# A decoder block with a 16384-expert mixer on one core: gates fetched and applied one tile further ahead, exponentials between weight copies, first two router heads sooner, low parts in two halves

## What is computed

```python
q = (xc @ wq).reshape(PEER_CHUNK, PEER_HEADS, 2, PEER_QDIM // 2)
sc = jnp.einsum('thpd,pkd->thpk', q, subkeys)
sv, si = lax.top_k(sc, PEER_TOPK)
cand = sv[:, :, 0, :, None] + sv[:, :, 1, None, :]
cv, ci = lax.top_k(cand.reshape(PEER_CHUNK, PEER_HEADS, PEER_TOPK * PEER_TOPK), PEER_TOPK)
i1 = jnp.take_along_axis(si[:, :, 0], ci // PEER_TOPK, axis=-1)
i2 = jnp.take_along_axis(si[:, :, 1], ci % PEER_TOPK, axis=-1)
e = i1 * PEER_NKEYS + i2
g = jax.nn.softmax(cv.astype(jnp.float32), axis=-1)
act = jax.nn.gelu(jnp.einsum('td,thkd->thk', xc, u[e]))
return jnp.einsum('thk,thkd->td', g * act, v[e])
```

## Time and profile before

| | us |
|---|---|
| timed runs, median (lowest to highest) | 1072.34 (1070.92 to 1072.85) |
| profiled execution | 1071.63 |
| its span | 1069.6 |
| PE busy / DVE / ACT / POOL | 1047.1 / 812.1 / 629.8 / 332.5 |
| U's tiles 0 to 127 start | 269.18 to 656.24 |
| V's tile 0 starts, `last_two` starts, last matmul starts | 660.11, 1058.50, 1066.00 |

### The profile page before, as it was taken

One profiled execution on the slowest core, in us unless ns is written; L12 is line 12 of the kernel. 1 busy time (PEld: TensorE's weight loads), 2 busy tenths in 40 slices (PEclk: granted clock), 3 DMA queues, 4 the chain that ended last, 5 costly groups with the idle time before them and its releaser, 6 DMA issues.

```text
span 1069.6 us, 21135 instructions
## 1 busy us (share of the span) xinstructions
PE 1047.1 (98%) x6814; PEld 913.8 (85%) x6814; DVE 812.1 (76%) x1631; ACT 629.8 (59%) x1128; POOL 332.5 (31%) x227
## 2 busy tenths in 40 slices
PE   9999999999999999999999999999999999999998
PEld 7798899999999999999999999766676777777775
DVE  7768886788989988977667667887778876666665
ACT  5557776665455445477667666666666654444443
POOL 0011211036268777876877874000000000000000
PEclk9999999999999999999999999999999999999999
DMA  8674646665456666576766766555555576666553
GB/s 339 245 236 134 203 142 212 197 205 170 157 161 174 173 182 188 166 187 168 176 165 169 177 159 173 178 176 169 168 172 177 177 228 200 202 201 201 199 200 106
DMA packets 89473, 198.20 MB, mean 185 GB/s; under 512 B 26320, under 2 KB 42832, under 8 KB 89424
## 3 DMA queue, kind: packets, MB, share of 16 engines
q1 hardware_dynamic: 68544, 188.99, 53.6%
q0 software_dynamic: 20736, 8.46, 6.9%
q10 hardware_dynamic: 144, 0.14, 0.1%
HBM read 187.01 MB, written 10.55 MB: 185 GB/s over the span
## 4 chain that ended last, share of the span: by engine, by line
PE 57%; DVE 15%; issue 14%; ACT 11%; DVEq 1%; ACTq 1%; DMA 0%
PE bank L830 10%; PE bank L832 10%; PE bank L831 10%; ACT hi L1197 7%; DVE lo L1682 6%; DVE big L1922 3%; ACT auxh L1224 3%; PE bank L384 2%; PE bank L385 2%; PE bank L386 2%; PE bank L450 2%; PE bank L770 2%; DVE gsum L1860 2%; DVE oneA L1852 2%; PE bank L454 1%
## 5 line engine op out<-in xcount | busy, mean ns | idle before, releaser
L1682 DVE TENSOR_TENSOR lo<-raw,hi 128x1024 fp32r<-128x1024 f32 x253 | 320.6, 1271 | 100.4 <-ACT hi L1197 99.7
L1197 ACT ACTIVATE hi<-raw 128x1024 fp32r<-128x1024 f32 x253 | 266.2, 1052 | 155.4 <-PE bank L832 152.4
L830 PE MATMUL bank<-xhi,hi 128*128 128x256 f32 x1024 | 292.4, 286 | 3.5 <-DVE lo L1682 2.3
L832 PE MATMUL bank<-xhi,lo 128*128 128x256 f32 x1024 | 290.6, 284 | 0.0
L831 PE MATMUL bank<-xlo,hi 128*128 128x256 f32 x1024 | 290.4, 284 | 0.0
L2038 POOL DMA_INDIRECT gate_d<-chosen_w,chosen_at x128 | 236.2, 1845 | 73.7 <-issue 48.2
L830 PEld LDWEIGHTS bank<-xhi,hi 128*128 128x128 f32 x1024 | 197.4, 193 | 4.0 <-ACT hi L1197 3.5
L831 PEld LDWEIGHTS bank<-xlo,hi 128*128 128x128 f32 x1024 | 197.2, 193 | 0.0
L832 PEld LDWEIGHTS bank<-xhi,lo 128*128 128x128 f32 x1024 | 197.0, 192 | 0.0
L886 PE MATMUL bank<-hi,auxh 128*128 128x512 f32 x504 | 168.3, 415 | 1.8 <-DVE auxl L1915 0.4
L886 PE MATMUL bank<-lo,auxh 128*128 128x512 f32 x504 | 156.9, 392 | 0.0
(11 more groups left out here) (393 smaller groups left out, 1493.2 us busy)
## 6 DMA issues: line engine op xcount, KB each, us to landing
raw<-u_d SPq DMA_DIRECT2D x128, 512.0 KB, 3.4
raw<-v_d SPq DMA_DIRECT2D x128, 512.0 KB, 3.4
raw<-wpre_d SPq DMA_DIRECT2D x70, 512.0 KB, 4.4
gate_d<-big POOLq DMA_DIRECT2D x16, 512.0 KB, 5.4
gring<-gate_d SPq DMA_DIRECT2D x128, 64.0 KB, 3.0
big<-wpre_d SPq DMA_DIRECT2D x8, 512.0 KB, 8.3
gate_d<-chosen_w,chosen_at POOLq DMA_INDIRECT x128
big<-x_d SPq DMA_DIRECT2D x4, 256.0 KB, 4.3
```

The costliest lines, as they stand in the source:

```text
L830: pe.matmul(out, wh, xhi[:, k, :], start=(k == 0), stop=False)
L832: m = pe.matmul(out, wl, xhi[:, k, :], start=False, stop=(k == KT - 1))
L1197: act.activation(hi[:, slot(n), :], raw[:, splits(n) % RING, :], ACT.Copy).then_inc(hi_done, 1)
L1682: dve.tensor_tensor(lo[:, slot(n), :], raw[:, splits(n) % RING, :], hi[:, slot(n), :].bitcast(F32), ALU.subtract).then_inc(lo_done, 1)
```

## The change

Five edits, in the order of the diff. The exponentials move to U's steps 4, 18 and 50 and are laid between the copies: table load, high part of one tile, exponential, high part of the next, table load, then the gelu of the pair. In DVE's router order the first two heads (8 and 9) go through `choose_pairs`, `numbers`, `weights` and `addresses` ahead of `choose_keys(15)` and `choose_keys(0)`. In U's second half each low part is subtracted in two halves of 512 columns. In V `gate_block` runs for block j + 4 in step j, not j + 3, with one more block ahead of the loop. POOL scatters five columns instead of three ahead of the pair sums of heads 14 and 15, and waits for their keys only behind these.

```diff
--- before.py
+++ after.py
@@ -67,7 +67,7 @@
 HALF = NBLK // 2
 GRING = 4
 EARLY = 7
-EXP_AT = (8, 20, 51)
+EXP_AT = (4, 18, 50)
 
 
 PARAMS = dict(g2=8, qg=64, kgc=64, kgs=128, posk=16, posv=16, w2k=128, w2v=128, subk=256, gw=192)
@@ -1251,11 +1251,15 @@
             act.wait_ge(S("h_saved"), 16 * TB)
             def weights_exp(z, b, c0, c1):
 
+                j = EXP_AT[z]
                 act.preload_act_table_set(LN_EXP)
+                loop_hi(0, N_PRE + j + SPLIT)
                 act.wait_ge(S("router_d"), z + 1)
                 of_heads = gwt[:, c0 * 16:c1 * 16]
                 act.activation(of_heads, of_heads, ACT.Exp, scale=rs2[:, b:b + 1]).then_inc(S("router_exp"), 1)
+                loop_hi(0, N_PRE + j + 1 + SPLIT)
                 act.preload_act_table_set(GELU)
+                gelu_pair(0, j + 1, 0)
 
             def u_steps(j0, j1):
 
@@ -1264,11 +1268,11 @@
 
             u_steps(0, EXP_AT[0])
             weights_exp(0, 1, NH, NH + 2)
-            u_steps(EXP_AT[0], EXP_AT[1])
+            u_steps(EXP_AT[0] + 2, EXP_AT[1])
             weights_exp(1, 1, NH + 2, 2 * NH)
-            u_steps(EXP_AT[1], EXP_AT[2])
+            u_steps(EXP_AT[1] + 2, EXP_AT[2])
             weights_exp(2, 0, 0, NH)
-            u_steps(EXP_AT[2], ROUTER - 2)
+            u_steps(EXP_AT[2] + 2, ROUTER - 2)
             for j in range(ROUTER - 2, ROUTER):
                 loop_hi(0, N_PRE + j + SPLIT)
             act.wait_ge(S("bank67_read"), 2)
@@ -1800,19 +1804,19 @@
 
             keys_ready()
             spread(1)
-            choose_keys(0)
             sc_out(NH - 1)
-            spread(2)
+            choose_pairs(NH, 4)
+            from_best(NH, NH + 2)
+            numbers(NH, NH + 2, 4, 6)
+            weights(0, NH, NH + 2)
+            dve.wait_ge(S("cleared"), 16 * 16)
+            addresses(NH, NH + 2)
             dve.wait_ge(S("sc_out"), NH)
             choose_keys(2 * NH - 1)
             keys_ready()
-            spread(3)
-            choose_pairs(NH, 6)
-            from_best(NH, NH + 2)
-            numbers(NH, NH + 2, 6, 9)
-            weights(0, NH, NH + 2)
-            dve.wait_ge(S("cleared"), 16 * 16)
-            addresses(NH, NH + 2)
+            spread(8)
+            choose_keys(0)
+            spread(9)
             for z in range(3):
                 choose_pairs(NH + 2 + 2 * z, 12 + 3 * z)
             from_best(NH + 2, 2 * NH)
@@ -1883,6 +1887,14 @@
             dve.wait_ge(S("bank45_read"), NH + HALF // 2)
             dve.tensor_copy(gsum[:, 0, 0:1], eT[:, 2, 0:1]).then_inc(S("weighed"), 1)
 
+            def loop_lo_halves(i, n):
+
+                dve.wait_ge(hi_done, i * UNROLL + splits(n + 1))
+                dve.tensor_tensor(lo[:, slot(n), 0:512], raw[:, splits(n) % RING, 0:512],
+                                  hi[:, slot(n), 0:512].bitcast(F32), ALU.subtract).then_inc(S("lo_first"), 1)
+                dve.tensor_tensor(lo[:, slot(n), 512:1024], raw[:, splits(n) % RING, 512:1024],
+                                  hi[:, slot(n), 512:1024].bitcast(F32), ALU.subtract).then_inc(lo_done, 1)
+
             def u_step_g(i, j):
                 g = j // 2
                 if j % 2 == 0:
@@ -1892,7 +1904,7 @@
                     weigh(i, g, GT)
                     rows_a(i, g + 2, GT)
                 if j < HALF - 1:
-                    loop_lo(i, N_PRE + HALF + j + SPLIT)
+                    loop_lo_halves(i, N_PRE + HALF + j + SPLIT)
 
             each_tile(dve, HALF - 16, u_step_g)
             for j in range(HALF - 16, HALF):
@@ -1928,6 +1940,7 @@
             gate_block(0, 1)
             w_lo_tokens(0, 1, "whi_done", 1, "wlo_done")
             gate_block(0, 2)
+            gate_block(0, 3)
             w_lo(0, 1)
             dve.wait_ge(S("bank45_read"), NH + NBLK // 2)
             weigh(0, NGRP, GT)
@@ -1937,7 +1950,7 @@
             def v_step(i, j):
                 w_lo(i, j + SPLIT - 1)
                 loop_lo(i, V0 + j + SPLIT)
-                gate_block(i, j + SPLIT)
+                gate_block(i, j + GRING)
 
             def v_step_g(i, j, keys=True, rows=True):
                 g = NGRP + 1 + j // 2
@@ -1951,12 +1964,14 @@
                     if rows:
                         rows_a(i, g + 2, GT)
                 loop_lo(i, V0 + j + SPLIT)
-                gate_block(i, j + SPLIT)
+                gate_block(i, j + GRING)
 
             each_tile(dve, HALF - 16, v_step_g)
             for j in range(HALF - 16, HALF - 2):
                 v_step_g(0, j, keys=j < HALF - 8, rows=j < HALF - 6)
-            each_tile(dve, HALF - 1, lambda i, j: v_step(i, HALF - 2 + j))
+            each_tile(dve, HALF - 2, lambda i, j: v_step(i, HALF - 2 + j))
+            w_lo(0, NBLK - 2)
+            loop_lo(0, V0 + NBLK - 1)
             w_lo(0, NBLK - 1)
             dve.wait_ge(S("h_back"), 16 * TB)
             for z, (b, c, w) in enumerate(out_parts_v):
@@ -2044,10 +2059,10 @@
                 pair_sum(c)
             pick(NH)
             pick(NH + 1)
-            pool.wait_ge(S("keys_chosen"), 2)
             pool.wait_ge(S("router"), 1)
             pool.wait_ge(S("chosen"), 1)
-            scatter(3)
+            scatter(5)
+            pool.wait_ge(S("keys_chosen"), 2)
             pair_sum(2 * NH - 2)
             pair_sum(2 * NH - 1)
             scatter(8)
```

## The result

The changed kernel takes 1026.14 us (median; 1025.43 to 1026.70, four runs), the kernel before, run beside it, 1072.59 us (1070.92 to 1073.77). The ratio is 0.9568, 95% interval 0.9551 to 0.9584: 46 us less. The profiled execution took 1025.43 us, its span 1023.6. Forecast were 1028 and a range of 1021 to 1040.

The account below looks back on a forecast made before the run. PE was taken to bound the kernel, busy 98% of the span, V's pairs lengthened by a DVE-ACT round trip. 38.8 + 1.9 + 3.3 = 44.0 us off 1072.34 gives 1028.3, said 1028; range 1021 to 1040.

Parts of the forecast that it names:

- What bounds the kernel: PE is busy 98% of the span; V's pairs take 6.90 us against 5.94 before the stalls begin.
- Part 1: V: making the gates one tile further ahead takes it from 398.4 to 359.6 us, saving 38.8 us.
- The wait that I left to DVE in even steps: V's first half: part of a wait can remain where squares_b stands before w_hi on ACT, 0.2 to 0.3 us.
- rival A: V's first half: DVE keeps one 0.69 us wait per pair, pairs of 6.2 us, 8 us lost, 1036 us; chance 0.14.
- The gate loads: V: gates needed three steps after sending, 8.2 us less about 1; landing 3.0, at most 5.6; cover 1.6 us.
- rival D: V: gate loads set the pace, step at least (L+1)/3 for landing time L; 1089 us at L=9; chance 0.03.
- the sign: V: whether the change gains or loses time turns at 3.2 us per tile, a gate landing time of 8.6 us.
- Part 2: V's end, last_two: the 1.93 us stall for the last tile's low weights goes, saving 1.9 us.
- Part 3: U's first half: first stall's 3.5 us goes, new 0.9 at tile 9, second shrinks by 0.7; 3.3 us saved.
- The lock rule: U, tile 9: the skill's Vector/GpSimd exclusion would give a stall of about 2.3 us; set aside for the row's 0.55 loss.
- Rival B: U: stalls at tile 9 (and 12) of 2 to 3 us with the half clock, 1032 us; chance 0.15.
- Part 4: U's second half: halves cost DVE 0.06 us more per tile, 4 to 10 us in all, hidden; taken as 0.

Follow-up runs that it names:

- gates_late2: The changed kernel with the gates of block j + 2, not j + 4, sent for in SP's step j; 1060.29 us, ratio 0.9898.
- gates_late1: The changed kernel with the gates of block j + 3, not j + 4, sent for in SP's step j; 1025.97 us.
- order_back: The changed kernel with the old router order on DVE and POOL, first exponential at step 8 but still between the copies; 1025.48 us.
- exps_back: The changed kernel with the exponentials as before (ahead of steps 8, 20, 51, table loads in a row); 1034.52 us, ratio 0.9646.
- the last two tries: The changed kernel with three low parts laid sooner in DVE's order, 1024.30 us; then also two scatters moved behind the pair sums of heads 6 and 7, 1024.35 us.
- only_gates: The kernel before with only the gates one tile further ahead and the reordered last tiles; 1028.78 us, ratio 0.9594.
- gates_back: The changed kernel with the gates-further-ahead edit undone and all the rest kept; 1068.04 us, ratio 0.9970.

## Why the prediction was right, point by point

**What bounds the kernel.** Right. V runs at the rate that its first, unstalled pairs showed: 5.92 us per pair for the 5.94 taken from the earlier trace rows.

**Part 1, V.** Right in mechanism, 1.3 us too small: 358.3 us for 359.6. The pair was taken 0.02 too long, the tile 0.01, thirty and sixty-five times over. The wait that I left to DVE in even steps is there, smaller than my 0.2 to 0.3 us (0.16 at 707.34). DVE's work was mis-sized, 5.24 us for 5.52. I took the period less the idle time; but consecutive instructions overlap by about 0.1 us, and behind a wait they don't, so a stretch with waits in it gives too much. It didn't matter here; for rival A it was the whole case: with 5.24 us of work one wait of 0.69 would have given pairs of 5.93, the PE's own period, and cost nothing.

**The gate loads.** The sum took nothing for them, rightly: they land in 1.9 to 5.7 us, median 3.0, and nobody waits. The law behind rival D was off by one step. With four steps and not three the changed kernel's ring stands, by my estimate from the rows of `gates_late2`, some 4 x 2.73 - 2.5 = 8.4 us of landing time before the PE notices (in V's first half 4 x 2.96 - 3.5 = 8.3), and by the same law 4 x 3.2 - 2.5 = 10.3 us and not 8.6 before the sign turns. The chance for D was too high, if anything. `gates_late1` and `gates_late2` bracket it. I also compared the traffic with the wrong window: the 172 GB/s were those of 500 to 550, 700 to 750 had 175. The 216 that I worked out for V are there, 200 in its first half and 215 in its second.

**Part 2, the end.** 2.3 us for 1.9. I took the bracket, 1.93; it counts from the end of a matmul that would have overlapped the next one. By the spacing of starts in the kernel before, 1059.04 to 1061.37 less 0.23, the wait was 2.10, and the first matmul behind it ran 0.07 longer, as did the one at 1058.50.

**Part 3, U.** The saving was 3.55 for 3.3, the stall at tile 9 was 0.60 for 0.9, the second 1.26 for 1.3, and no half clock. That the 1.6 us of half clock could be counted in full was luck in part: it doesn't follow in every execution (see the end). And the reason was half wrong. The old first stall was, with the old router order kept, already down to 0.43 us once the table loads stood elsewhere (`order_back`); I gave it to DVE's `choose_pairs`. And I called the exponential safe because `router_d` is there before ACT comes to it; I never asked the reverse, who waits for `router_exp`. DVE does, in `weights`, with two low parts queued behind. In the change ACT is early, so the sum was right; `exps_back` shows what the missing question costs, 8.4 us.

**The lock rule.** I set it aside, and was wrong to. The 2.53 us of the earlier trace rows are two multiplications merged in one row, and I took them for two of 1.27. One by one they are

```profile
292.03 0.86 POOL L2028 TENSOR_TENSOR big<-big 128x256 f32<-128x256 f32 x1 [1.30 <-DVE big L1776]
...
292.84 1.72 POOL L2028 TENSOR_TENSOR big<-big 128x256 f32<-128x256 f32 x1
```

The first takes 0.86 us. The low part that begins at 292.20 finds 0.64 of that left and loses 0.55; the second multiplication, beside the low part, takes twice as long as the first. The rule of the Trainium skill (SBUF — State Buffer, section "SBUF: two separate sides") has whichever starts first hold the ports for its whole length and the other wait, and the rows agree with it, as the scatters do above. What failed was my reading of it: a copy waits for the rest of the multiplication under way, not for a whole one, so the rule asks for the same 0.55 us as the row and not for a stall of 2.3. In the changed kernel the low part beside the multiplications takes 1.73 us and the stall is 0.60. Rival B, 2 to 3 us of stall with the half clock, did not come.

**Part 4, halves.** Right: hidden. Its price for DVE is 1.07 us per 50, or 0.07 per tile of 3.1 us, for the 0.06 put. The last scatter starts 13.6 us sooner than before (639.28 for 652.85), more than V's start does, as said; that some of it comes from the halves I had not seen.

## What to carry to other kernels

A value that one engine makes and another rounds for the first again costs a round trip in each step; making it one step further ahead took one more instruction ahead of the loop and a slot that was already there, and gave 43 of 46 us. Before a step with a wait is moved, ask both questions: is its input there, and who waits for its output. Where a row merges several instructions, take them apart before you read a duration from it. Take an engine's work from the spacing of rows that stand back to back, not from a period less its waits; and count for a load's cover the steps of the whole ring, from the wait back to the wait, by the order in which the waiting engine does its work.

## What the runs showed that I had not expected

The last store lands either 2.4 or 3.7 us after the last addition, and not in between. From the start of the last addition (0.69 us long) to the end of the span are 3.1 to 3.2 us in nine of the fourteen profiled executions and 4.4 to 4.5 in five, among them both ways for the same kernel. The last addition starts at 1020.49 in the changed kernel's first profile (span 1023.6) and at 1021.41 in its second (span 1025.9): 3.1 and 4.5 us. That is 1.3 us of scatter that no engine's work explains, and as much as the last two tries were worth; with a few runs each, a gain below it is better read from the last addition than from the median. What decides between the two was not tried.

The length of a stall doesn't settle what clock follows it. Windows from the first matmul behind a stall on, of `only_gates` (the stall of 1.88 us by its bracket, 2.04 by spacing):

```profile
307.60:312.00 4.40, 4.40 (x24) 4.40 (x25) 4.40 (x14) 0.00 (x0) 4.10 (x4) 0.61 0.67 207
```

And of the changed kernel, behind its 0.60:

```profile
296.68:301.00 4.32, 4.32 (x36) 4.32 (x37) 4.32 (x18) 1.83 (x3) 3.71 (x3) 1.00 0.73 211
```

After 2.04 us the clock was 0.61 over 24 matmuls, after the 5.4 us of `exps_back` 0.50 over 28, after 0.60 it was 1.00. But in the kernel before the 2.10 us in `last_two` cost no clock: the matmuls behind it follow at 0.23 us, as the same ones do in the changed kernel. Yet `gates_back`, which has the same stall in `last_two` at the same length (1055.01 to 1057.34 less 0.23), pays for it. Its row and the window behind it:

```profile
1057.34 0.57 PE L901 MATMUL bank<-hi,auxh 128*128 128x512 f32 x1 [1.93 <-DVE auxl L1920]
...
1057.56:1061.00 3.44, 3.44 (x9) 2.65 (x9) 0.69 (x1) 0.00 (x0) 0.00 (x0) 0.50 0.17 64
```

The matmuls there follow at 0.43 us, and `last_two` up to its last matmul takes 9.1 us for 7.5. So the same code with the same stall can go either way. The runs' mean clocks say the same: of the 32 timed runs of the kernel before beside the experiments six have 1.000 (1068.55 to 1069.62 us), fifteen 0.998 (1070.21 to 1072.43) and eleven 0.997 (1072.15 to 1073.42), and `only_gates`, with the stall in U alone, has 1.000 once (1027.19) and 0.998 three times (1028.74 to 1029.59). The changed kernel, whose stalls are 0.9 us or less, has 1.000 in all nine of its runs. So a stall of 2 us costs the kernel some 1.6 us more in most executions and nothing in others; what decides it stays open. Up to 3 us of the 46 hang on that, and it was luck in part that the forecast, which counts one such stretch, met the median.
